# Decoder layer with PEER experts on one core: 32 of 256 tokens leave the dense expert-U product and are gathered row by row

## The reference, cut to what matters

```
s1, s2 = q1 @ keys[0].T, q2 @ keys[1].T        # 8 heads, 128 keys each
idx    = the 16 best of 256 pairs of the 16 best of each  # 16 experts a head
g      = softmax(their scores)
h      = einsum('chkd,cd->chk', U[idx], x)      # 128 experts a token
a      = g * gelu(h)
y      = einsum('chk,chkd->cd', a, V[idx])
```

## Time and profile before

| | |
|---|---|
| median of 3 runs | 2451.82 us (2450.42 to 2453.93) |
| profiled execution | 2451.64 us |
| its span | 2449.9 us |
| TensorE busy | 2365.1 us |
| VectorE busy | 1609.7 us |
| ScalarE busy | 1108.7 us |
| GpSimd busy | 586.9 us |
| read from memory, written | 451.77 MB, 21.10 MB |

### The profile page before, as it was taken

How to read it: one execution, slowest core, us unless ns; L and a number is a source line. 1 busy time by engine, 2 the same in 40 slices (tenths; PEclk the granted TensorE clock), 3 DMA queues, 4 the chain that set the end, 5 groups by cost and what they waited for, 6 DMA issues and landing times.

```text
span 2449.9 us, 46109 instructions
## 1 busy us (share of the span) xinstructions
PE 2365.1 (97%) x14762; PEld 2145.6 (88%) x14762; DVE 1609.7 (66%) x2433; ACT 1108.7 (45%) x1715; POOL 586.9 (24%) x360
## 2 busy tenths in 40 slices
PE   7999999999899899999999999999899999999996
PEld 7988799877897699899999999999788888888885
DVE  4444566655534645799999999998455555555556
ACT  3444455643433343345444445444344444444442
POOL 0000000000201016777466655565200000000000
PEclk9999999999899999999999999999999999999998
DMA  8787555465344565677777777776766666666664
GB/s 316 248 281 263 174 154 153 140 241 195 131 155 148 163 166 109 149 182 182 182 181 180 181 183 183 182 181 171 256 215 217 216 217 219 216 214 220 221 212 139
DMA packets 326826, 473.77 MB, mean 193 GB/s; under 512 B 66768, under 2 KB 214480, under 8 KB 323440
## 3 DMA queue, kind: packets, MB, share of 16 engines
q1 hardware_dynamic: 284704, 444.71, 58.7%
q0 software_dynamic: 41360, 27.54, 6.9%
q10 hardware_dynamic: 704, 0.75, 0.1%
HBM read 451.77 MB, written 21.10 MB: 193 GB/s over the span
## 4 chain that ended last, share of the span: by engine, by line
PE 94%; DVE 2%; DMA 1%; ACT 1%; issue 1%; POOL 0%; SPq 0%; DVEq 0%; ACTq 0%; POOLq 0%
PE ps L648 29%; PE ps L670 28%; PE ps L437 18%; PE ps L443 15%; PE ps L637 2%; DMA temps<-gates_scratch 1%; PE ps L585 1%; PE ps L603 1%; DMA weight_ring<-in_w_in_dram 0%; DVE split_ring L1146 0%; PE ps L621 0%; PE ps L418 0%; ACT parts L731 0%; ACT split_ring L748 0%; PE ps L516 0%
## 5 line engine op out<-in xcount | busy, mean ns | idle before, releaser
L648 PE MATMUL ps<-parts,u_hi 128*128 128x256 f32 x3904 | 705.8, 284 | 4.3 <-DVE u_lo L1359 4.2
L648 PEld LDWEIGHTS ps<-parts,u_hi 128*128 128x128 f32 x3904 | 609.6, 192 | 7.0 <-DVE u_lo L1359 7.0
L1146 DVE TENSOR_TENSOR split_ring<-weight_ring,split_ring 128x1024 fp32r<-128x1024 f32 x288 | 353.1, 1233 | 363.9 <-ACT split_ring L748 355.1
L1110 POOL DMA_INDIRECT gates_scratch<-sb_gains x256 | 501.9, 1960 | 312.3 <-ACT sb_gains L885 191.3
L670 PE MATMUL ps<-parts,temp_parts 128*128 128x512 f32 x2304 | 547.8, 391 | 6.3 <-DVE parts L1496 6.3
L648 PE MATMUL ps<-parts,u_lo 128*128 128x256 f32 x1952 | 552.9, 283 | 0.0
L670 PEld LDWEIGHTS ps<-parts,temp_parts 128*128 128x128 f32 x2304 | 435.2, 189 | 98.4 <-DVE parts L1496 7.5
L748 ACT ACTIVATE split_ring<-weight_ring 128x1024 fp32r<-128x1024 f32 x288 | 302.8, 1059 | 367.0 <-PE ps L437 226.1
L437 PE MATMUL ps<-split_ring,parts 128*128 128x512 f32 x1920 | 439.9, 391 | 5.6 <-DVE parts L1262 3.9
L1496 DVE TENSOR_TENSOR parts<-region,parts 128x512 fp32r<-128x512 f32 x384 | 253.1, 687 | 285.0 <-ACT parts L987 284.8
L437 PEld LDWEIGHTS ps<-split_ring,parts 128*128 128x128 f32 x1920 | 360.8, 188 | 81.0 <-DVE split_ring L1146 4.1
(11 more groups left out here) (200 smaller groups left out, 1364.3 us busy)
## 6 DMA issues: line engine op xcount, KB each, us to landing
u_raw<-in_peer_u_dram SPq DMA_DIRECT2D x1024, 128.0 KB
region<-in_peer_v_dram SPq DMA_DIRECT2D x256, 512.0 KB, 4.1
weight_ring<-in_w_in_dram SPq DMA_DIRECT2D x96, 512.0 KB, 4.9
weight_ring<-in_w_mkv_dram SPq DMA_DIRECT2D x64, 512.0 KB, 3.8
gates_scratch<-temps POOLq DMA_DIRECT2D x16, 1024.0 KB, 7.2
weight_ring<-in_w_o_dram SPq DMA_DIRECT2D x32, 512.0 KB, 3.7
weight_ring<-in_w_mq_dram SPq DMA_DIRECT2D x32, 512.0 KB, 3.7
weight_ring<-in_w_mo_dram SPq DMA_DIRECT2D x32, 512.0 KB, 3.6
```

The lines of the kernel that those rows point to most:

```text
L648: m = nc.tensor.matmul(ps[:, b, 0:T], u[:, c], x[kk], start=kk == 0 and n == 0, stop=kk == KB - 1 and n == 2)
L1110: pool.indirect_dma_start(gates_by_one, bass.IndirectOffsetOnAxis(ap=idx_all[:, j:j + 1], axis=0), gate_all[:, j:j + 1], None, compute_op= ...
L1146: nc.vector.tensor_tensor(w_lo[j % SPLIT], raw[j % RAW], w_hi[j % SPLIT].bitcast(F32), ALU.subtract).then_inc(lo_ready, 1)
```

## The change

32 tokens, the last 32 of 256, leave the dense U product: its matmuls get 224 columns (`ET = T - PICKED`), native and split, and so do `E`, the gate loads and the products on `E`. For the V product the parts of E stay 256 columns wide; GpSimd fills the last 32 with zeros once, so the V matmuls are unchanged.

The 32 tokens have 128 experts each, 4096 pairs of a token and an expert, which are laid out as 32 columns by 128 partitions (four groups of 32 partitions for the experts, 32 tokens in each). For each column GpSimd gathers 128 rows of U (1 MB) by an indirect DMA into one of four buffers, and VectorE multiplies it by the tokens' x and sums it to one number a partition (`dot_line`, 128x2048). Dots stand behind the blocks 6, 8, ..., 68 of the V stage. Behind block 71 ScalarE takes gelu of the 128x32 sums, VectorE multiplies by the gates. Then for each column 128 rows of V are gathered and added with their weight to a 128x2048 sum (`add_line`), behind the blocks 74, 75, 77, 78, 80, ... 123. Four matmuls with a matrix of ones and zeros (`fold`) add the sum's four groups of partitions into PSUM ahead of the last block.

Besides:
- The twelve rounds keep all their blocks split (`PLAIN` is empty). TensorE's loop over them has 9 blocks a body instead of 3.
- The two `DENSE` searches are written out instead of looped, and in the second one u_hi and u_lo of the first split units are made between the steps.
- `HOME` is reordered, `MOVED` is 3 instead of 2: E is smaller and regions 0, 1, 3 and 5 stay free behind it.
- SyncE writes x of the 32 tokens to memory (8 DMAs); GpSimd reads it back to four groups of partitions at the start of V, in place of x2, gain and bias, which are now loaded between gathers, from the 45th of 64 on.
- VectorE's loop over the V blocks is written out.
- GpSimd waits for the key products and makes `fold` ahead of its first scatter.

```diff
-        E = at("experts", 0, NKEY * T)
+        E = at("experts", 0, NKEY * ET)
...
-            def split_unit(i, h, slot, b):
-                pe.wait_ge(u_lo_ready, i * 2 + (h + 1 - NATIVE))
+            def split_unit(rank, h, slot, b):
+                pe.wait_ge(u_lo_ready, rank + (h + 1))
...
-                        m = nc.tensor.matmul(ps[:, b, 0:T], u[:, c], x[kk], start=kk == 0 and n == 0,
+                        m = nc.tensor.matmul(ps[:, b, 0:ET], u[:, c], x[kk][:, 0:ET], start=kk == 0 and n == 0,
...
             mix_block(NKEY - 2, 0)
+            pe.wait_ge(fold_set, 5)
+            pe.wait_ge(line_used, LINES)
+            for q in range(4):
+                nc.tensor.matmul(ps[:, 4 + q, :], fold, line_sum[:, q * BANK:(q + 1) * BANK], start=False, stop=False,
+                                 skip_group_check=True)
...
-            with act.Fori(0, DENSE) as m:
+            for m in range(DENSE):
                 n = m + EARLY
+                last = m == DENSE - 1
                 copy_scores(n, tk_first)
                 for b in range(3):
                     take_hidden(m * 3 + b, b)
                     if b == 1:
                         gate_exps(n, tk_first)
+                        if last:
+                            for u in range(NATIVE, NATIVE + 2):
+                                unit_hi(u, u % US)
...
+            for j in range(4):
+                pool.dma_start(x2_four[32 * j:32 * j + 32, :], picked_dram).then_inc(x2_four_landed, 16)
+            pool.wait_ge(pick_landed, 128)
+            for c in range(LINES):
+                if c >= 4:
+                    pool.wait_ge(line_used, c - 3)
+                carry_wait()
+                k = c % PICKED
+                pool.indirect_dma_start(lines[c % 4], None, (peer_u if c < PICKED else peer_v)[0],
+                                        bass.IndirectOffsetOnAxis(ap=line_of[:, k:k + 1], axis=0)).then_inc(line_landed[c % 4], 16)
+                if c == LINES // 2 + 12:
+                    pool.wait_ge(e_lo_ready, 64)
+                    pool.dma_start(gain3_b, ln3_g[0].partition_broadcast(P)).then_inc(gb_landed, 16)
+                    pool.dma_start(bias3_b, ln3_b[0].partition_broadcast(P)).then_inc(gb_landed, 16)
+                if LINES // 2 + 12 <= c < LINES // 2 + 28:
...
                     pool.dma_start(dst, src).then_inc(x2_landed, 16)
...
+                    elif m == DENSE - 1 and k in (12, 14):
+                        u = NATIVE + (k - 12) // 2
+                        unit_lo(u - NATIVE, u % US)
...
+            def dot_line(c):
+                if c == 0:
+                    dve.wait_ge(x2_four_landed, 64)
+                line_here(c)
+                nc.vector.tensor_tensor_reduce(lines[c % 4], lines[c % 4], x2_four, 1.0, 0.0, ALU.mult, ALU.add,
+                                               line_dot[:, c:c + 1]).then_inc(line_used, 1)
+
+            def add_line(c):
+                line_here(LINES // 2 + c)
...
+                    dve.wait_ge(line_used, LINES // 2 + c)
+                    m = nc.vector.scalar_tensor_tensor(out=line_sum, in0=lines[c % 4], scalar=line_dot[:, c:c + 1],
+                                                       in1=line_sum, op0=ALU.mult, op1=ALU.add)
+                m.then_inc(line_used, 1)
+
+            for i in range(NKEY):
+                rests(i, i % 2, last=i == NKEY - 1)
+                if i in dot_after:
+                    dot_line(dot_after[i])
...
+                if i in add_after:
+                    add_line(add_after[i])
```

More of the change, by code:

```diff
@@ L156, in layer_program, with split_rank, is_split @@
         EARLY, DENSE = 2, 2
-        SPREAD, MOVED = SEARCHES - EARLY - DENSE, 2
+        SPREAD, MOVED = SEARCHES - EARLY - DENSE, 3
         NATIVE = 6 * DENSE
         PER = 18
+        PLAIN = ()
+        PICKED = 32
+        ET = T - PICKED
+        LINES = 2 * P * PICKED // P
+        dot_after = {6 + 2 * c: c for c in range(LINES // 2)}
+        ACTED = 72
+        add_after = {ACTED + 2 + c * 8 // 5: c for c in range(LINES // 2)}
+        def split_rank(y):
+            body, y = y // PER, y % PER
+            return body * (PER - 2 * len(PLAIN)) + y - 2 * sum(2 * b + 1 < y for b in PLAIN)
+        def is_split(y):
+            return y % PER // 2 not in PLAIN
         u_raw = [at(f"u_raw{s}", HOME[5] + s * UW, UW) for s in range(US)]
@@ L174, in layer_program @@
         g_ring = [ta[:, 5120 + s * T:5120 + (s + 1) * T] for s in range(2)]
-        gain3_b, bias3_b = ta[:, 0:D], ta[:, D:2 * D]
-        x2_back = rows(r1)
+        x2_back, y_out = rows(at("x2_back", 0, RC)), rows(at("y_out", RC, RC))
+        ends = at("last_gain_bias", 2 * RC, 2 * D)
+        gain3_b, bias3_b = ends[:, 0:D], ends[:, D:2 * D]
+        lines = [r0[:, s * D:(s + 1) * D] for s in range(2)] + [ta[:, s * D:(s + 1) * D] for s in range(2)]
+        x2_four, line_sum = r1[:, 0:D], r1[:, D:2 * D]
         def by_mixed(a):
@@ L688, in mix_block @@
                         pe.wait_ge(e_lo_ready, i + 1)
+                    if first and q == 0:
+                        pe.wait_ge(pad_set, 1)
                     if first and q == 1:
@@ L1007, in _ @@
             v_parts(0, 1)
-            with act.Fori(1, NKEY // 2 - 1) as pair:
+            with act.Fori(1, ACTED // 2) as pair:
+                for b in range(2):
+                    v_parts(pair, b)
+            act.wait_ge(line_used, LINES // 2)
+            nc.scalar.activation(line_act, line_dot, ACT.Gelu).then_inc(line_acted, 1)
+            with act.Fori(ACTED // 2, NKEY // 2 - 1) as pair:
                 for b in range(2):
@@ new lines, in _ @@
+            for j in range(4):
+                to, of = slice(32 * j, 32 * j + 32), slice(P - PICKED, P)
+                pool.dma_start(line_of[to], pick_of[of, 32 * j:32 * j + 32]).then_inc(pick_landed, 16)
+                pool.dma_start(line_gate[to], gate_all[of, P + 32 * j:P + 32 * j + 32]).then_inc(pick_landed, 16)
+            pool.wait_ge(u_used, UNITS - 1)
+            for e in e_hi + e_lo:
+                m = pool.memset(e[:, ET:T].bitcast(F32), 0.0)
+            m.then_inc(pad_set, 1)
@@ L1463, in spread_search @@
                 search(m + (EARLY + DENSE), tk, lambda k: turn_and_lo(PER - 15 + k, m, steps.wait))
-            for u in range(NATIVE, NATIVE + 2):
-                unit_lo(u, u % US)
             for first, end, tk in ((0, SPREAD - MOVED, tk_first), (SPREAD - MOVED, SPREAD, tk_last)):
```

135 lines of the change are left out of this document (86 added, 49 removed).

## The result

The kernel after took 2455.97 us (median of 11 runs, 2451.14 to 2467.03), the kernel before beside it 2450.42 (11 runs, 2449.35 to 2453.93): ratio 1.0023, 95% interval 1.0014 to 1.0032. The forecast was 2439, faster. The profiled execution took 2451.61 us (span 2449.5), near the fastest of its runs, so it is set against the profile of before (span 2449.9).

What follows compares the result with a forecast made beforehand. TensorE, busy for 97% of the span, was taken as the bound, with VectorE close behind in the U stage. 2451.6 us less 42 in U plus 29 in V gave 2439 us, range 2415 to 2474.

Steps and rivals of the forecast that it cites:

- Native blocks and handover: U stage: 192 narrower native instructions save 5.0 us; preparing the first split units earlier saves 5.3 us.
- Split matmul: U stage: 224 columns take 107 ns a matmul instead of 120.5; the 28 units without search gain 8.8 us.
- Rival (a): Split U matmuls stay at the 256-column cost because the weight load sets the pace: 2470 us, chance 0.15.
- Rounds: U stage's twelve rounds: VectorE comes next as bound, each takes 50.1 us instead of 52.0, saving 22.8 us.
- Lines in V: V stage: each of 64 dots and additions on VectorE overruns its slack by 0.36 us, adding 23 us.
- slack of 1.92 us: V stage: time from v_lo of quarter 0 being ready to TensorE's use, 1.92 us with the narrower e_lo.
- Rival (b): V stage: the 32 sums with an accumulator run at half rate on VectorE: 2506 us, chance 0.06.
- Gates "now and then late: +4 us": V stage: gather packets delay V halves or gate loads by about 2.5 us, adding 4 us for the whole stage.
- Rival (c): V stage: DMA engines become the bound, with 314 GB/s as ceiling: +33 us, 2472 us, chance 0.10.
- Opening: Start of V stage: x2, last gain and bias leave, gathers and x2 rows come: -1 us, bounds -6 and +5.
- Fold: Ahead of the last V block: four native matmuls over 512 columns, 8 instructions, add 3.4 us.

Runs made afterwards that it cites:

- second profile: The changed kernel run once more, unedited, and profiled again: 2453.75 us, ratio 1.0011.
- gap kernel with early gates: Changed kernel, dot and addition operations moved between v_lo of quarters 1 and 2, next block's gates issued between the V halves: 2425.31 us, ratio 0.9897.

## Why the prediction was wrong, by its steps

**Native blocks and handover: right.** 41.4 us became 36.3 (-5.1, forecast -5.0), and the gap and the slow clock behind it are gone: the gap shrank by 4.0 us and the first split unit from 4.22 to 3.19 us, for a forecast 5.3 in all. The first split unit starts 9.7 us earlier in this profile (forecast 10.3 in all), and 5 to 10 earlier over all kernels with 224 columns, since what comes before varies; from the first native matmul it is 9.1 in each of the two profiles.

**Split matmul: the step "32 columns less are 13.3 ns, so 107.2 ns a matmul" failed.** It is 111.7: the straight line through 256 and 512 columns does not go on, since from 240 columns down the load of 128 weight columns sets the pace (by the runs with 192 and 240 columns and with 64 weight columns). Rival (a) had the cause right and the size wrong: it held the pace at 120. No row at hand gave the number. The native group of 128 columns at 112 ns looks like it, but native matmuls take 216 ns at 256 columns, 189 at 224 and 163 at 192 (the kernel with 192 columns), a line that comes to 110 at 128: there the 112 ns can as well be the columns' own. It shows that a load can come every 112 ns, as the prediction said, and not that it can't come faster. The prediction took 107 all the same, a faster load than the row shows. The step took 3.8 us from the tail (28 x (2.70 - 2.88) = -5.0, forecast -8.8).

**Rounds: right in mechanism.** VectorE sets them, 50.38 us for a forecast 50.1; measured 12 x (50.38 - 52.10) = -20.6 against -22.8. The part of TensorE's slots rose with the matmul. U as a whole: -36.1 instead of -42.

**Lines in V: right in mechanism, slightly too cheap.** 0.40 us a dot for 0.36, and 12.7 us for 32 dots (forecast 11.5), shown by taking the gathers away (12.7 stays) and the lines away (0.0). An addition takes 2.27 us start to start and costs 0.44: 14.2. Together 26.9 for 23. A dot is shorter than forecast (2.21 for 2.28) and costs more, so the term that was off is the slack of 1.92 us: it is 2.21 - 0.40 = 1.81. (A slack larger by 0.2 us would have given +10 us, 64 x 0.16, and not the +8 of the prediction.) Rival (b) fell: the sum with an accumulator is recorded at 2284 ns, full rate, and its read at 82. The Trainium skill ("Vector Engine (DVE) Microarchitecture Reference", "Points that are easy to get wrong") would halve the rate for two such sources; the addition's 2346 ns for 2048 columns disagree, as the 1278 for 1024 did.

**Gates "now and then late: +4 us": failed in size.** The additions' stretch lost 19.0 us in one profile and 23.5 in the other, so 4.8 and 9.3 above the lines' 14.2. A single 10 us block makes the difference. This is also the part of the runs' spread that the two profiles show. The step that was left out: the prediction counts it as a gain that x2, gain and bias leave the opening, and puts nothing for where they go, and block 89, right behind gain and bias, has 4.1 of the 4.8 us. Rival (c), a ceiling of 314 GB/s, fell: 61 us of the additions' stretch ran at 339 GB/s, and in the gap kernel with early gates the dots at 309 cost nothing.

```profile
2143.00:2204.00 61.00, 57.87 (x246) 45.56 (x245) 45.68 (x69) 26.48 (x52) 10.45 (x10) 0.99 0.92 339
```

**Opening: -1 us, measured +0.7 and +1.3.** About the same bytes did not make the burst shorter. **Fold:** 3.0 for 3.4.

V in all: 26.9 + 4.8 + 0.7 + 3.0 = 35.4 for a measured 35.8 (second profile: 26.9 + 9.3 + 1.3 + 3.0 = 40.5 for 41.0), forecast 29. The forecast's gain of 13 was the difference of two sums of 42 and 29; 6 us missing on the one and 7 to 12 on the other take it to zero and below. The split matmul is the largest miss (6.0 us with the rounds), then the lines (3.9) and the opening (1.7 and 2.3); the late gates add 0.8 in the first profile and 5.3 in the second. No term alone turned the sign. The median of the second set of runs is 0.1% over before, ratio 1.0011. That the first median is 5.5 us over before while the first profile equals it lies in the spread; which executions lose more was seen in two profiles only.

Left open: why gathers and the loads of x2, gain and bias, each nearly free alone, make gates late together (the stretches with the losses ran at 321 GB/s, the dots' at 308), and whether the V half or the gather delays the gates. With the line in the gap and early gates the loss among the additions is 6.9 us, with these loads moved and the lines spread besides 0.5, but the last two edits were not separated.

## What to carry to other kernels

Before counting on a narrower matmul that brings its own weights, ask what its weight load takes: a line through wider shapes says nothing of it, and a narrower group in the trace shows only that a load can come that fast. One run with the narrow width alone would have priced it here. Work added to a nearly idle engine costs its overrun past the next thing that has a due time; put it in the gap, but first see which loads its new place brings forward and which small load stands behind them: here the same line in the same gap was worth +1.5% or, with one DMA issue moved, -1.0%. When loads leave one stage, price them where they arrive. Where a forecast is a small difference of two large sums, its sign is no safer than the worst term.

## What the runs showed of the hardware

- fp32r matmuls with 128 weight columns: 227.1 ns at 512 columns, 120.5 at 256, 111.7 at 240, 224 and 192; at most 89.5 ns at 192 columns with 64 weight columns. The record of a load is 192 ns for 128 columns and 135 for 64, longer than the pace: the records overlap.
- Native float32 with 128 weight columns: 216 ns an instruction at 256 columns, 189 at 224, 163 at 192, 112 at 128.
- VectorE: a subtraction of float32 into fp32r over 128x1024 takes 1183 ns, a copy of float32 into fp32r of that size 653.
- A 112 KB load issued behind a 512 KB one and a gather of 1 MB made VectorE wait 54 times, 113.6 us in all, at a DMA share of 0.79 and 274 GB/s among the dots; issued ahead of them, 4 times and 4.6 us, at 0.88 and 309 GB/s.
- Behind a gap of 4.24 us TensorE's granted clock was 0.50 for over 2 us; behind one of 0.24 us it stayed at 1.00.
